# First couple of experts in the others' order, and the narrow experts' weights loaded from ScalarE's queue

## The reference

```python
def moe_swiglu(x, w_router, b_router, wg, wu, wd):
    logits = (x @ w_router) + b_router
    top_v, top_i = lax.top_k(logits, 2)
    top_w = jax.nn.softmax(top_v, axis=-1)
    combine = sum(one_hot(top_i, 8) * top_w[..., None], axis=-2)
    for e in range(8):
        out += combine[..., e:e+1] * (silu(x @ wg[e]) * (x @ wu[e])) @ wd[e]
```

## Time and profile before

| | us |
|---|---|
| Median of 3 runs | 1285.68 (1284.71 to 1286.19) |
| Profiled execution, its own time | 1287.22 |
| Its span | 1285.1 |
| TensorE busy | 1232.7 (96%) |
| VectorE busy | 766.0 (60%) |
| ScalarE busy | 594.9 (46%) |
| Mean granted clock | 0.991 |

### The profile page before, as it was taken

The page is one execution under the profiler, slowest core; times in us unless marked ns, Lnnn a source line. Parts: engine busy times, 40 slices in busy tenths (PEclk is TensorE's granted clock), DMA queues, the critical chain, the costliest instruction groups (busy, mean ns, idle before and its releaser), DMA issues.

```text
span 1285.1 us, 16075 instructions
## 1 busy us (share of the span) xinstructions
PE 1232.7 (96%) x6377; PEld 888.9 (69%) x6377; DVE 766.0 (60%) x818; ACT 594.9 (46%) x571; POOL 92.0 (7%) x109
## 2 busy tenths in 40 slices
PE   7989999999999999999999998999998999999996
PEld 6987888887987865656656666656665666666662
DVE  5888645448888856545555555654653555565643
ACT  5555434444554535454434445545444444445521
POOL 1660000000660000000000000000000000000000
PEclk9999999999999899999999999999999999999998
DMA  9737655554336779999999999999999999999994
GB/s 318 274 104 242 217 179 185 196 179 149 132 111 205 286 254 420 421 419 419 420 403 421 420 419 418 419 419 412 420 419 419 420 419 411 419 419 419 419 418 168
DMA packets 88496, 425.07 MB, mean 331 GB/s; under 512 B 9520, under 2 KB 11856, under 8 KB 76128
## 3 DMA queue, kind: packets, MB, share of 16 engines
q1 hardware_dynamic: 87056, 420.21, 82.8%
q0 software_dynamic: 1216, 3.71, 1.1%
q10 hardware_dynamic: 144, 0.07, 0.0%
HBM read 422.91 MB, written 1.05 MB: 330 GB/s over the span
## 4 chain that ended last, share of the span: by engine, by line
PE 66%; DMA 15%; DVE 11%; issue 4%; ACT 4%; SPq 0%; DVEq 0%; ACTq 0%
PE bank L1765 16%; PE bank L1767 15%; PE bank L1766 15%; PE bank L2144 8%; PE bank L2138 6%; DMA raw<-in_wd_exp 5%; DVE w_lo L1163 3%; DMA raw<-in_wu_exp 3%; DMA raw<-in_wg_exp 2%; ACT w_hi L822 2%; DVE arena L1267 1%; DMA arena<-in_wd_exp 1%; DMA tokens<-in_wu_exp 1%; DVE w_lo L1186 1%; DMA tokens<-in_wg_exp 1%
## 5 line engine op out<-in xcount | busy, mean ns | idle before, releaser
L1765 PE MATMUL bank<-w_hi,parts 128*128 128x512 f32 x888 | 341.6, 385 | 23.5 <-DVE w_lo L1163 19.0
L1163 DVE TENSOR_TENSOR w_lo<-raw,w_hi 128x1792 fp32r<-128x1792 f32 (+1 forms) x130 | 271.0, 2101 | 134.3 <-ACT w_hi L822 120.8
L1766 PE MATMUL bank<-w_lo,parts 128*128 128x512 f32 x888 | 335.4, 378 | 0.0
L1767 PE MATMUL bank<-w_hi,parts 128*128 128x512 f32 x888 | 334.4, 377 | 0.0
L822 ACT CAST w_hi<-raw 128x1792 fp32r<-128x1792 f32 (+1 forms) x130 | 227.4, 1758 | 116.6 <-DMA raw<-in_wg_exp 43.2
L1765 PEld LDWEIGHTS bank<-w_hi,parts 128*128 128x128 f32 x888 | 168.3, 190 | 76.0 <-issue 38.1
L1767 PEld LDWEIGHTS bank<-w_hi,parts 128*128 128x128 f32 x888 | 168.0, 189 | 31.8
L1766 PEld LDWEIGHTS bank<-w_lo,parts 128*128 128x128 f32 x888 | 168.8, 190 | 29.0
L1186 DVE TENSOR_TENSOR w_lo<-raw,w_hi 128x2048 fp32r<-128x2048 f32 x60 | 138.6, 2312 | 60.1 <-PE bank L1767 46.3
L842 ACT CAST w_hi<-raw 128x2048 fp32r<-128x2048 f32 x60 | 114.0, 1910 | 75.3 <-PE bank L1767 65.7
L2144 PE MATMUL bank<-raw,arena 128*64 128x512 f32 (+1 forms) x704 | 137.4, 541 | 0.0
(11 more groups left out here) (266 smaller groups left out, 1234.3 us busy)
## 6 DMA issues: line engine op xcount, KB each, us to landing
raw<-in_wu_exp SPq DMA_DIRECT2D x91, 896.0 KB, 15.1
raw<-in_wg_exp SPq DMA_DIRECT2D x89, 896.0 KB, 15.3
raw<-in_wd_exp SPq DMA_DIRECT2D x77, 1024.0 KB, 16.3
arena<-in_wd_exp SPq DMA_DIRECT2D x23, 1024.0 KB, 17.9
arena<-in_wg_exp SPq DMA_DIRECT2D x26, 896.0 KB, 14.7
arena<-in_wu_exp SPq DMA_DIRECT2D x24, 896.0 KB, 13.9
raw<-in_w_in SPq DMA_DIRECT2D x20, 1024.0 KB, 5.8
tokens<-in_wd_exp SPq DMA_DIRECT2D x12, 1024.0 KB, 15.4
```

The lines of the kernel that those rows point to most:

```text
L1163: v.tensor_tensor(low(o)[:, 0:w], ring[s][:, 0:w], high(o)[:, 0:w].bitcast(F32), ALU.subtract) \
L1765: mm(psum, left[0], right[0], start=first, stop=False)
L1766: mm(psum, left[0], right[1], start=False, stop=False)
L1767: return mm(psum, left[1], right[0], start=False, stop=last)
```

## The change

The first block gets the order of the others: A gate, B gate, A up, B up, A down, B down, with the wide turn after the third B up unit, PSUM banks 0 to 3 for its wide gate units (so TensorE waits for the count, which is read from bank 1, before the first of them), and bank 7 for the gather of the narrow tokens.

The first loads are now wide gate 0 to 6, wide up 0 to 2, wide gate 7, wide up 3, and narrow gate 0. Each later unit takes the ring buffer whose unit is the earliest in the order (`place_units`), which from unit 30 on is again unit n-10.

From the second couple on (p of 1 and more), the narrow units are issued by ScalarE's queue: at unit n, ahead of its cast of unit n+3, ScalarE waits for the release of the buffer and issues unit n+8. SyncE's queue issues the wide units, and both streams of the first couple.

```diff
@@ block_phases
-    if (p, b) == (0, 0):
-        return [("A", "g", g), ("A", "u", g), ("B", "g", g), ("B", "u", g), ("A", "d", d), ("B", "d", d)]
@@ turned_a_after
-    if (p, b) == (0, 0):
-        return "B", "g", 2
@@
-FIRST_SLOTS = [*range(RAW), ESG_SLOT, RAW, *EH_SLOTS, RAW + 1, RAW + 2]
-LEAD = len(FIRST_SLOTS)
-FIRST_LOADS = [*range(RAW), 8, 9, 10, 7, 11, 12]
-SLOT = [FIRST_SLOTS[n] if n < LEAD else (n - LEAD) % RING for n in range(N_UNITS)]
-USE = [SLOT[:n].count(s) for n, s in enumerate(SLOT)]
-def slot_before(n):
-    return max(m for m in range(n) if SLOT[m] == SLOT[n])
+UA0 = AT[0, 0, "A", "u", 0]
+FIRST_SLOT = {**{n: n for n in range(RAW)}, UA0: RAW, UA0 + 1: EH_SLOTS[0], UA0 + 2: EH_SLOTS[1], RAW: ESG_SLOT,
+              UA0 + 3: RAW + 1, GATE_UNITS: RAW + 2}
+LOADS = list(FIRST_SLOT) + [n for n in range(N_UNITS) if n not in FIRST_SLOT]
+def place_units():
+    slot, use, before, times = {}, {}, {}, [0] * (RING + 3)
+    holds = {}
+    for n in LOADS:
+        s = FIRST_SLOT[n] if n in FIRST_SLOT else min(holds, key=lambda r: holds[r])
+        slot[n], before[n], use[n] = s, holds.get(s), times[s]
+        times[s] += 1
+        if s < RING:
+            holds[s] = n
+    return slot, use, before, times
+SLOT, USE, BEFORE, USES = place_units()
+ACT_LEAD = RING - 2
+ACT_LOADS = {n for n, u in enumerate(UNITS) if u[0] and u[2] == "B"}
@@ SyncE
-            for n in FIRST_LOADS + list(range(LEAD, N_UNITS)):
+            for n in LOADS:
+                if n in ACT_LOADS:
+                    continue
...
@@ ScalarE
+            def load_narrow(n):
+                p, b, stream, kind, q = UNITS[n]
+                if p not in narrow_expert:
+                    if not narrow_expert:
+                        act.wait_ge(order_ready, 1)
+                    at_e = 2 * p + 3
+                    narrow_expert[p] = act.value_load(order_int[0:1, at_e:at_e + 1], min_val=0, max_val=E - 1)
+                if BEFORE[n] in ORDINAL:
+                    act.wait_ge(lo_ready, split_count(ORDINAL[BEFORE[n]]))
+                else:
+                    act.wait_ge(unit_done, done(BEFORE[n]))
...
+                act.dma_start(dst, src).then_inc(landing(n)[0], 16)
             def experts():
                 for n, (p, b, stream, kind, q) in enumerate(UNITS):
+                    if n + ACT_LEAD in ACT_LOADS:
+                        load_narrow(n + ACT_LEAD)
                     if n and n + HI_AHEAD < N_UNITS:
                         round_expert(n + HI_AHEAD)
@@ TensorE, start_phase
                     if i == 0:
                         pe.wait_ge(xg_ready, 2)
                         pe.wait_ge(xgfirst_ready, 2)
+                        pe.wait_ge(count_ready, 1)
...
                 elif (stream, kind) == ("A", "u"):
-                    if i == 0:
-                        pe.wait_ge(xgn_first, 1)
-                        pe.wait_ge(count_ready, 1)
-                    else:
-                        pe.wait_ge(esilu, 2 * i + 1)
+                    pe.wait_ge(esilu, 2 * i + 1)
                 elif (stream, kind) == ("B", "g"):
                     if i == 0:
-                        pe.wait_ge(esilu, 1)
+                        pe.wait_ge(xgn_first, 1)
```

More of the change, by code:

```diff
@@ L164 @@
 ESG_SLOT, EH_SLOTS = RING, (RING + 1, RING + 2)
-FIRST_SLOTS = [*range(RAW), ESG_SLOT, RAW, *EH_SLOTS, RAW + 1, RAW + 2]
-LEAD = len(FIRST_SLOTS)
-FIRST_LOADS = [*range(RAW), 8, 9, 10, 7, 11, 12]
-assert sorted(FIRST_LOADS) == list(range(LEAD)) and LEAD <= 2 * GATE_UNITS
-SLOT = [FIRST_SLOTS[n] if n < LEAD else (n - LEAD) % RING for n in range(N_UNITS)]
-USE = [SLOT[:n].count(s) for n, s in enumerate(SLOT)]
-def slot_before(n):
-    return max(m for m in range(n) if SLOT[m] == SLOT[n])
+UA0 = AT[0, 0, "A", "u", 0]
+FIRST_SLOT = {**{n: n for n in range(RAW)}, UA0: RAW, UA0 + 1: EH_SLOTS[0], UA0 + 2: EH_SLOTS[1], RAW: ESG_SLOT,
+              UA0 + 3: RAW + 1, GATE_UNITS: RAW + 2}
+LOADS = list(FIRST_SLOT) + [n for n in range(N_UNITS) if n not in FIRST_SLOT]
+assert RAW < GATE_UNITS
+def place_units():
[11 more added lines that the diff above has]
+ACT_LOADS = {n for n, u in enumerate(UNITS) if u[0] and u[2] == "B"}
+assert all(m is None or m < n for n, m in BEFORE.items())
 C_ID, C_TRI, C_ONES = 0, 128, 256
@@ L381, in build @@
         landed = [sem(f"landed{n}") for n in range(RAW)]
-        fetched = [sem(f"fetched{n}") for n in range(len(FIRST_SLOTS))]
+        fetched = [sem(f"fetched{n}") for n in range(RING + 3)]
         x_in = [sem(f"x_in{t}") for t in range(TT)]
@@ L465, in build @@
         FIRST_BANKS = ((4, 6), (5, 7))
-        FIRST_B_BANK = 3
+        FIRST_B_BANK = 7
         TAIL_BANKS = (2, 3, 0, 1)
         SCATTER_BANKS = (4, 5, 7, 6)
-        WORK_A, FIRST_A, GATE_B, UP_B = 0, 4, 4, 6
+        WORK_A, GATE_B, UP_B = 0, 4, 6
         FILLS = EXP_BLOCKS * 4
@@ L539, in build @@
             + [esg, eh_raw[:, 0, :], eh_raw[:, 1, :]]
-        assert len(ring) == len(FIRST_SLOTS)
+        assert len(ring) == RING + 3
         def done(n):
@@ L599, in landing_extra @@
             return fetched[s], j * (16 * len(range(s, ITEM_UNITS, RING))) + 16 * (
-                SLOT.count(s) + u // RING + 1)
+                USES[s] + u // RING + 1)
         def width_of(kind):
@@ L664, in _ @@
                     experts[p, stream] = order_at(slice(at_e, at_e + 1))
-                if n >= LEAD:
-                    if slot_before(n) in ORDINAL:
-                        sp.wait_ge(lo_ready, split_count(ORDINAL[slot_before(n)]))
+                if n not in FIRST_SLOT:
+                    if BEFORE[n] in ORDINAL:
+                        sp.wait_ge(lo_ready, split_count(ORDINAL[BEFORE[n]]))
                     else:
-                        sp.wait_ge(unit_done, done(slot_before(n)))
+                        sp.wait_ge(unit_done, done(BEFORE[n]))
                 elif n < RAW:
@@ L1060, in hidden_narrow @@
                        wide_bank(GATE_B, EHALF).rearrange("p (c h t) -> p h c t", h=2, t=NARROW)).then_inc(ehn_ready, 1)
+            narrow_expert = {}
+            def load_narrow(n):
[5 more added lines that the diff above has]
+                    narrow_expert[p] = act.value_load(order_int[0:1, at_e:at_e + 1], min_val=0, max_val=E - 1)
+                if BEFORE[n] in ORDINAL:
+                    act.wait_ge(lo_ready, split_count(ORDINAL[BEFORE[n]]))
+                else:
+                    act.wait_ge(unit_done, done(BEFORE[n]))
+                dst, src = ring[SLOT[n]][:, 0:width_of(kind)], expert_source(kind, b, q, narrow_expert[p])
+                if len(src.shape) == 3:
+                    dst = dst.rearrange("p (k n) -> p k n", n=src.shape[2])
+                act.dma_start(dst, src).then_inc(landing(n)[0], 16)
             def experts():
@@ L1071, in experts @@
                             act.wait_ge(eturn_a, 4 * i)
-                        gate_silu(wide_pieces(esg, wide_bank(WORK_A if i else FIRST_A, EBLK)))
+                        gate_silu(wide_pieces(esg, wide_bank(WORK_A, EBLK)))
                     if step == ("B", "g", GATE_UNITS - 1):
@@ L2173, in start_phase @@
                 elif (stream, kind) == ("A", "u"):
+                    pe.wait_ge(esilu, 2 * i + 1)
+                elif (stream, kind) == ("B", "g"):
                     if i == 0:
                         pe.wait_ge(xgn_first, 1)
-                        pe.wait_ge(count_ready, 1)
-                    else:
-                        pe.wait_ge(esilu, 2 * i + 1)
-                elif (stream, kind) == ("B", "g"):
-                    if i == 0:
-                        pe.wait_ge(esilu, 1)
                     else:
@@ L2202, in experts @@
                     if stream == "A":
-                        unit_wide(ORDINAL[n], split_count(ORDINAL[n]), kind, q, WORK_A if i or kind == "u" else FIRST_A)
+                        unit_wide(ORDINAL[n], split_count(ORDINAL[n]), kind, q, WORK_A)
                     else:
```

## The result

The changed kernel takes 1293.03 us (median of 7 runs, 1291.24 to 1297.89), the kernel before 1285.88 in the same comparison (7 runs, 1284.71 to 1286.44). The ratio is 1.0062, with a 95% interval of 1.0048 to 1.0076: slower by 0.6%. The forecast was 1282.1, faster, with a range up to 1292.0. Sign and size were wrong.

The account below looks back on a forecast made before the run. Transfers were taken to lead TensorE by only 6 us a couple (210 against 204), so both matter. From 1285.7 us, -8.2 for the first couple's order and +4.6 for two queues gave 1282.1 us, range 1274.5 to 1292.

Parts of the forecast that it names:

- What bounds the kernel: Steady part: transfers need 210 us a couple, TensorE 204; up to about 480 us transfers are not the limit.
- Part one: First couple's new order: narrow gate units ahead of wide up units close later load gaps, -8.2 us.
- The bounds (1.1 to 8.7): Limits on the first couple's gain: 8.7 us by the transfers' lead, 1.1 if second-block waits turn into others.
- Part two: Two queues from the second couple on: same bytes, 138 loads moved to ScalarE's queue, landings reordered, +4.6 us.
- rival (a): Landing order is kept, or reordering costs nothing, so only the first couple's gain counts: 1277.5 us, chance 0.27.
- rival (b): Side-by-side service starves TensorE at each phase's end and only one old wait goes: 12.6 us, 1290.1 us, chance 0.23.
- the 7.0 us of stalls in a couple: Second couple, late landings: wide down units 2.8, next block's wide gates 1.3, narrow gates 2.9 us.
- The old waits: Two TensorE waits in the second couple, 2.7 and up to 3.1 us, expected to go as wide units come earlier.
- What was priced at nothing: ScalarE's 138 issues at 0.33 us each, and its loads going out up to 7 us later: no cost expected.
- The tail: From 1219.30 us on, TensorE's own chain and then the last norm's: nothing changes.
- The dry stretch: First couple's stretch of low transfers, at share 0.26 from 442 to 456 us, expected to move to 442 to 453.
- a dip of the transfers in each couple: Named sign of a wrong prediction: transfers dipping longer than 1 us in each couple.
- (c): First couple's lead is lost in its second block by full buffers or lower clock: 1284.6 to 1289.2 us, chance 0.10.

Follow-up runs that it names:

- experiment 1: Changed kernel with its new first-couple order but all loads issued by SyncE's queue: 1278.96 us, ratio 0.9955 to the kernel before.
- experiment 3: Changed kernel with all loads on SyncE's queue, issued in the order and as late as with two queues: 1279.46 us, ratio 0.9957 to the kernel before.
- experiment 6: Changed kernel with only the 42 narrow down units of the later couples on ScalarE's queue: 1299.45 us, ratio 1.0091 to the kernel before.

## Why the prediction was wrong, step by step

**What bounds the kernel: right.** The transfers move 418 GB/s from 500 to 1250 us with one queue (experiment 1), 412 after, and TensorE has some 6 us of slack in a couple. That slack was too small to take what followed.

**Part one, -8.2: right in kind, 2.8 too large.** Counted from the end of the wide gate units (449.8 there, 447.11 here), its marks hold to 0.1 us as far as the second block's wide up units: end of the first narrow up units 45.7 expected and 45.7 measured, third wide down unit 52.0 and 52.0, second block 78.5 and 78.5, wide up units 110.2 and 110.2. Then the wide down units were expected at 143.6 and began at 145.8, and the third at 150.1, against 152.7: the wide up units took 20.06 instead of 19.4, and TensorE waited 1.48 and 0.49 us behind landings which the text had as early enough. That the difference at 597.54 ends just where the prediction put it (599.9) is chance: the 2.65 us that the profiled execution before was late hide the 2.6 lost here. The bounds (1.1 to 8.7) hold 5.4. Of these, 4.1 are waits (six with 6.3 us before, three with 2.2 after, from the end of the wide gate units to the second couple) and 1.4 TensorE's busy time. Behind the wait of 3.18 at 565.26, which the new order removes, the clock before was 0.72 in 565 to 569; the prediction's sum had no term for it.

**Part two, +4.6: this is where it failed.** Side-by-side service was rightly preferred to first come, first served, and so rival (a) fell; experiment 3 is how (a) would have gone. "Each unit that is served early is missing nothing later", written against rival (b), is the sentence that was wrong. The term is the 7.0 us of stalls in a couple. It looked for units pushed back by those issued to ScalarE's queue ahead of the end of a wide phase (2.8, measured 1.5), of the next wide gates (1.3, measured none) and of the narrow gates (2.9, measured 0.3), 1.8 in place of 7.0. It left out that the wide units overtake the last narrow ones in the same way: 4.0 us at the narrow up units of the two blocks, 2.0 at the narrow down units, 0.8 ahead of the second block's last wide down units, 6.8 together. The old waits did go, 5.4 us of them by the timeline where 5.8 were taken. 8.6 - 5.4 = 3.2. The other 1.5 of the step's 4.8 are in TensorE's busy time (207.40 us after, 205.85 before, over the couple); phases with a wait inside are 0.2 to 0.4 longer than without even when the wait is taken off. Experiment 1 has 207.16, but with the stretch at 0.60 in it; without that it would be about 205.6, as before. What makes the couples with two queues 1.5 us busier at full clock stays open. That the last couple costs about as much as the others (4.5, expected 2) has the same reason.

**What was priced at nothing.** ScalarE's issue time and its later sending: right as far as the runs tell, by experiment 3 for the lateness and by experiment 6 for the number of loads. The tail: the last mark to the end of the span is 46.3 us after and 46.4 before (1285.1 - 1238.74), right.

**Signs named.** The dry stretch moved as said: 40% share and 122 GB/s from 440 to 450 us, 93% and 349 from 450 to 460. The waits of TensorE on narrow landings are there. What the text called a sign of error, a dip of the transfers in each couple, is there too:

```profile
864.00:884.00 20.00, 20.00 (x98) 9.80 (x97) 7.48 (x6) 7.32 (x7) 0.00 (x0) 1.00 0.84 326
...
1076.00:1096.00 20.00, 20.00 (x98) 11.10 (x98) 9.55 (x8) 6.63 (x6) 0.00 (x0) 1.00 0.83 322
```

These are the busy times by stretches after; with one queue (experiment 1) the same stretches move 402 and 411 GB/s, before 405 and 404. A late TensorE frees buffers late, and at the start of a couple nothing is left to move. This reading is argued from the rows, not shown by a run of its own. The transfers at full rate could have taken the loss back only if they had been the slower side throughout; they lead by 6 us a couple, and each dip gives some 4 us of that away (20 us at 326 instead of 405).

**The rivals.** (b), side-by-side service starving TensorE at the ends of the phases, is what happened, at 4.7 us a couple instead of its 4.2, and at 0.23 it had too small a chance. (c) named a lower granted clock as the way to lose the first couple's lead; in fact the clock had been lower before the change, in the profile on which all sums were built (it lies 1.5 us above the median of its runs).

## What to carry to other kernels

In this kernel, loads that are consumed in a fixed order belong in one queue as long as there is a backlog: the second queue brought no bytes, gave up that order, and let new units for later pass old ones that were wanted next. When two queues are weighed, look for overtaking in both directions at every change of phase, not only at the queue that gets the new loads. And read the granted clock of the stretches ahead of the change before its marks are compared: a start that differs by 2.65 us between executions looked like a part of the gain, and what looked like one split doing more harm than another was partly a lower clock behind longer waits.

## What was not expected of the hardware

- A load issued 1.4 us after another of its size (1024 KB), to a queue without backlog, landed 10.1 us ahead of it; with both in one queue, 2.7 us apart at issue, they landed 2.5 us apart in order.
- The queues share evenly only while both hold loads: 49.6% and 51.9% of the engines' time from 755 to 763 us after. From 734 to 742 ScalarE's queue, to which nothing was issued from 718.5 to 739.1, took 3.8% and SyncE's 97.8%; from 750 to 758, behind a pause of SyncE's issues from 734.1 to 750.9, it was 78.2% and 23.3%.
- Taking a third of the narrow loads to the second queue cost as much as taking all of them and more (17.5 us against 13.8 over experiment 1, by the ratios), with TensorE's waits in the second couple no longer (8.4 and 8.6 us) but its clock lower behind them (0.57 and 0.58 over 4 us each, against 1.00).
- The granted clock in the first wide gate units differs between executions of code that is the same there (0.72 to 1.00 in 442 to 448 us), and moved everything behind by 2.5 us.
